# Gated-MLP layers of a six-layer transformer on one core: seven half products for three of the projections' parts, layer norm sums on ScalarE, token mixing between the gate tiles

## The reference, cut to what matters

```python
def gmlp_mixer(h, w_in, ln_g, ln_b, w_s, b_s, w_out):
    B, S, _ = h.shape
    z = jax.nn.gelu(h @ w_in)
    u, v = jnp.split(z, 2, axis=-1)
    v = layernorm(v, ln_g, ln_b)
    n = S // GM_CHUNK
    v = v.reshape(B, n, GM_CHUNK, GM_GROUPS, GM_GROUP_DIM)
    mask = jnp.tril(jnp.ones((GM_CHUNK, GM_CHUNK), dtype=bool))
    ws = jnp.where(mask[None], w_s, jnp.zeros_like(w_s))
    sv = jnp.einsum('gts,bnsgd->bntgd', ws, v) + b_s.T[None, None, :, :, None]
    y = u * sv.reshape(B, S, GM_INNER)
    return y @ w_out
```

## Time and profile before

| | |
|---|---|
| median of 3 runs | 2519.59 us (2516.25 to 2520.73) |
| the profiled execution's own time | 2514.01 us |
| its span, first to last instruction | 2512.2 us |
| granted TensorE clock, mean | 0.993 of full |
| PE busy | 2410.5 us, 96% |
| PE's weight loads (PEld) busy | 2040.0 us, 81% |
| DVE busy | 1620.1 us, 64% |
| ACT busy | 528.1 us, 21% |

### The profile page before, as it was taken

One profiled execution on the slowest core, in us unless ns is written; L12 is line 12 of the kernel. 1 busy time (PEld: TensorE's weight loads), 2 busy tenths in 40 slices (PEclk: granted clock), 3 DMA queues, 4 the chain that ended last, 5 costly groups with the idle time before them and its releaser, 6 DMA issues.

```text
span 2512.2 us, 40482 instructions
## 1 busy us (share of the span) xinstructions
PE 2410.5 (96%) x15728; PEld 2040.0 (81%) x15728; DVE 1620.1 (64%) x3367; ACT 528.1 (21%) x1345; POOL 110.9 (4%) x212
## 2 busy tenths in 40 slices
PE   7998999998889999999999799999999999999997
PEld 4466999654669996789998589998789996789997
DVE  4755887447558873426995559964849983425773
ACT  2232010125321102102211322212222212102210
POOL 0000001000000000000110001110001110000000
PEclk9999999999999999999999999999999999999999
DMA  6223557531136565435876158874238874434442
GB/s 238 104 101 131 194 209 261 202 112 34 59 104 228 209 248 195 161 124 204 294 269 241 51 184 291 288 269 151 92 101 314 288 279 162 172 119 143 167 160 68
DMA packets 122363, 453.46 MB, mean 181 GB/s; under 512 B 13776, under 2 KB 13904, under 8 KB 121680
## 3 DMA queue, kind: packets, MB, share of 16 engines
q1 hardware_dynamic: 92880, 338.24, 38.1%
q0 software_dynamic: 29312, 112.80, 12.6%
HBM read 449.93 MB, written 1.05 MB: 180 GB/s over the span
## 4 chain that ended last, share of the span: by engine, by line
PE 85%; DVE 9%; ACT 3%; issue 2%; DMA 2%; SPq 0%; POOL 0%; DVEq 0%; ACTq 0%
PE pair L543 59%; PE bank L543 24%; DVE adat L1836 1%; DMA adat<-adaw_dram 1%; DVE att_s L1693 1%; PE bank L829 1%; DVE arena L1688 1%; ACT arena L1210 1%; ACT arena L1222 1%; DVE rstd L1472 1%; DVE h L1475 1%; DVE arena L1780 0%; PE bank L774 0%; DVE arena L2171 0%; DVE arena L2167 0%
## 5 line engine op out<-in xcount | busy, mean ns | idle before, releaser
L543 PE MATMUL pair<-h,ring 128*128 128x256 f32 (+1 forms) x3424 | 639.4, 346 | 9.3 <-issue 4.8
L543 PEld LDWEIGHTS pair<-h,ring 128*128 128x128 f32 x3424 | 567.6, 190 | 71.4 <-issue 7.2
L543 PE MATMUL pair<-arena,ring 128*128 128x128 f32 (+1 forms) x2476 | 388.5, 316 | 4.0 <-issue 2.8
L543 PEld LDWEIGHTS pair<-arena,ring 128*128 128x128 f32 x2476 | 355.2, 193 | 32.1 <-issue 4.4
L543 PE MATMUL bank<-arena 128*128 128x128 f32 (+2 forms) x2584 | 298.0, 279 | 32.7 <-ACT arena L1222 26.6
L543 PEld LDWEIGHTS bank<-arena 128*128 128x128 f32 (+2 forms) x2584 | 274.3, 185 | 67.4 <-ACT arena L1222 36.4
L543 PE MATMUL pair<-ring,h 128*128 128x512 f32 (+1 forms) x768 | 326.1, 582 | 3.0 <-DVE h L1475 3.0
L543 PE MATMUL pair<-arena 128*128 128x128 f32 (+6 forms) x2530 | 300.5, 283 | 8.1 <-ACT arena L1194 3.6
L543 PEld LDWEIGHTS pair<-arena 128*128 128x128 f32 (+4 forms) x2530 | 262.5, 185 | 40.9 <-issue 20.5
L543 PEld LDWEIGHTS pair<-ring,h 128*128 128x128 f32 x768 | 142.1, 191 | 168.5 <-issue 159.8
L1836 DVE CUSTOM_DVE_ANT_0 adat<-adat,crow,cols 128x1024 f32<-128x1024 f32 x192 | 244.2, 1278 | 50.0 <-DMA adat<-adaw_dram 50.0
(11 more groups left out here) (232 smaller groups left out, 2162.1 us busy)
## 6 DMA issues: line engine op xcount, KB each, us to landing
ring<-stream_dram SPq DMA_DIRECT2D x638, 512.0 KB, 4.4
adat<-adaw_dram POOLq DMA_DIRECT2D x192, 512.0 KB, 5.1
arena<-gmrows_dram POOLq DMA_DIRECT2D x2, 2560.0 KB, 11.1
arena<-cmpw_dram POOLq DMA_DIRECT2D x1, 2112.0 KB, 9.4
x<-x_in_dram SPq DMA_DIRECT2D x2, 512.0 KB, 4.6
arena<-mem_in_dram SPq DMA_DIRECT2D x1, 1024.0 KB, 12.5
arena<-gmws_dram POOLq DMA_DIRECT2D x2, 512.0 KB, 13.1
out_dram<-h POOLq DMA_DIRECT2D x2, 512.0 KB, 3.8
```

What stands on the lines that cost most here:

```text
L543: return nc.tensor.matmul(out, lhsT, rhs, start=start, stop=stop)
```

## The change

- `gm_v` is of a new kind "V" (`panels`): its first four tiles as before, but taken out of PSUM by ACT, with Gelu and a running sum (`accum_out`) in one; the other twelve as three panels of four tiles, each seven products of four matmuls of 256 columns, on banks 5, 6, 7 and 3. DVE makes four weight sums of 1024 elements a panel and puts the panel together (`panel_out`); ACT copies the first product and applies Gelu with sums.
- The layer norm's sums come from ACT: Gelu's running sums, then four `Square` instructions of 1024 elements with the mean as bias (`deviations`). DVE keeps the small reductions and four passes of 2048 elements.
- `gm_u`: tiles 0 to 3, 14 and 15 as before, 4 to 13 as five pairs (`GM_PAIRED`).
- `gm_out`: three pairs and the tail of two tiles.
- The mixing goes in eight groups of two feature tiles (four matmuls, a whole bank) and stands between gate tiles. DVE's `mixed` (an addition, then a product, of 512 elements each) stands behind each pair's combination and the weight sums two pairs on.

```diff
+            plan += [Linear(f"gm_v{i}", "V", DK, 16, "act"), Linear(f"gm_u{i}", "S", DK, 16, "act"),
+                     Linear(f"gm_out{i}", "S", 16, DK, "dve")]
...
+PANEL = [5, 6, 7, 3]
+GM_PAIRED = range(4, 14, 2)
...
+        GM_MB = (2, 4)
```

PE, in `panels`, for each of the three panels:

```diff
+                    if u == 0:
+                        bank_free(g)
+                    else:
+                        pe.wait_ge(sem("panel_read"), q)
+                    product(5, 0, lambda j: h[:, 2 * j, HALVES[0]], given(0, 0), t)
+                    product(5, 1, lambda j: h[:, 2 * j + 1, HALVES[0]], given(0, 1)).then_inc(sem("panel_first"), 1)
+                    if u == 0:
+                        pe.wait_ge(sem("moving_summed"), MOVING_SUMS[name] + 1)
+                    else:
+                        pe.wait_ge(sem("freed_dve"), FREER[g - 1][1])
+                    product(3, 1, lambda j: upT[1][:, 3, j, :], given(1, 1))
+                    pe.wait_ge(sem("panel_summed"), q + 1)
+                    product(6, 0, lambda j: upT[1][:, 1, j, :], summed(1), t + 4 * lin.K)
+                    product(7, 0, lambda j: upT[1][:, 0, j, :], summed(0))
+                    product(7, 1, lambda j: upT[1][:, 2, j, :], summed(2)).then_inc(sem("panel_mid"), 1)
+                    product(3, 0, lambda j: h[:, 2 * j + 1, HALVES[1]], summed(3)).then_inc(sem("mm_done"), 1)
```

PE, the mixing between gate tiles:

```diff
+                        def mix(m):
+
+                            if m == 0:
+                                pe.wait_ge(sem("gm_v_normed"), 1 + n3)
+                            if m >= 2:
+                                pe.wait_ge(sem("gm_mix_read"), GM_GROUPS * n3 + m - 1)
...
+                            for m in {5: (0,), 7: (1, 2), 9: (3,), 11: (4,), 13: (5,), 15: (6, 7)}.get(n, ()):
+                                mix(m)
```

DVE:

```diff
+                        for u, (_, g) in enumerate(lin.panels):
+                            panel_out(u, g)
+                            if u == 0:
+                                panel_weights(2)
...
+                        V.tensor_scalar(mean, total, -1.0 / GM_INNER, None, ALU.mult).then_inc(sem("gm_mean"), 1)
+                        up_weights()
+                        up_weights()
+                        dve.wait_ge(sem("gm_sq"), 4 * (1 + n3))
...
+                        for p, (_, _, g) in enumerate(lin.pairs):
+                            if p >= 2:
+                                dve.wait_ge(sem("gm_gated"), len(lin.pairs) * n3 + p - 1)
+                            combined(g, high[:, p % 2]).then_inc(sem("freed_dve"), 1)
+                            if p + 2 < len(lin.pairs):
+                                up_weights()
+                            for m in ((), (0,), (1, 2), (3,), (4,))[p]:
+                                mixed(m)
+                        down_weights(f"gm_out{i}")
+                        down_weights(f"gm_out{i}")
+                        mixed(5)
+                        mixed_sums(0)
+                        down_weights(f"gm_out{i}")
+                        down_weights(f"gm_out{i}")
+                        mixed(6)
+                        mixed(7)
+                        mixed_sums(1)
+                        residual(f"gm_out{i}", f"ffn2_{i}", gain, gate, None, high)
```

More of the change, by code:

```diff
@@ L466, in build @@
         for lin in PLAN.values():
-            if lin.kind == "S":
+            if lin.kind == "V":
+                MOVING_SUMS[lin.name] = n_sums
+                n_sums += 1
+            if lin.kind == "S" and not lin.name.startswith("gm_u"):
                 MOVING_SUMS[lin.name] = n_sums
@@ L627, in linear, with panels, product, given @@
                         t += lin.K * w
-            def seven(name, moving, sums, ready, sums_done, norm=None):
+            def panels(name, ready):
+                lin = PLAN[name]
+                t, g = lin.tile0, lin.g0
+                for tt in range(TT):
+                    bank_free(g + tt)
+                    for k in range(lin.K):
+                        ready(tt, k, 0)
+                        last = mm(banks[USED[g + tt][0]][:, :], h[:, k, HALVES[tt]], tile(t + 4 * k, 4), k == 0,
+                                  k == lin.K - 1)
+                        release(last, tt == 1 and k < lin.K - 1, t + 4 * k)
+                    last.then_inc(sem("mm_done"), 1)
+                for u, (t, g) in enumerate(lin.panels):
+                    q = u + len(lin.panels) * (name != "gm_v0")
+                    own = panelW[u % 2]
+                    def product(bank, slot, move, weights, free=None):
+                        for j in range(lin.K // 2):
+                            ins = mm(banks[bank][:, slot * TOK:slot * TOK + TOK], move(j), weights(j), j == 0,
+                                     j == lin.K // 2 - 1)
+                            if j == 0 and free is not None:
+                                release(ins, True, free)
+                        return ins
+                    def given(a, e):
+                        return lambda j: tile(t + (2 * a + e) * lin.K + 2 * j, 2)
+                    def summed(m):
+                        return lambda j: own[:, m, 2 * j:2 * j + 2, :].rearrange("p a q -> p (a q)")
+                    if u == 0:
[14 more added lines that the diff above has]
+                    product(3, 0, lambda j: h[:, 2 * j + 1, HALVES[1]], summed(3)).then_inc(sem("mm_done"), 1)
@@ L631, in seven @@
+            def seven(name, moving, sums, ready, sums_done, norm=None, after=None):
                 lin = PLAN[name]
@@ L725, in seven @@
                     t += lin.K * len(ns)
+                    if after is not None:
+                        after(ns[-1])
             def norm_part(name, k):
```

216 lines of the change are left out of this document (149 added, 67 removed).

## The result

| | before | after |
|---|---|---|
| median of 16 runs each, same chip | 2517.53 us (2514.51 to 2523.21) | 2523.34 us (2518.49 to 2527.62) |
| span of the profiled execution | 2512.2 us | 2522.8 us |
| granted TensorE clock, mean | 0.993 | 0.986 |
| first gated-MLP layer | 165.13 us | 166.70 us |
| second gated-MLP layer | 165.13 us | 167.42 us |

A forecast was written before the change was run, and what follows sets the result against it. PE was taken to bound the layers. Per layer, 18.0 us less work against 15.3 us of waits gave -5.4 us in two layers; clock falls added 11.0, so +5.6 on 2519.6: 2525.2 us, range 2511 to 2532.

The forecast's parts named there:

- PE work: Shorter matmul work: value panels 4.9 us, gate tiles 3.3, output tiles 3.9, mixing 5.9; 18.0 us less a layer.
- panels' waits: Value stage: panels 2 and 3 each wait 0.4 us for DVE's `panel_read`, 0.8 us a layer.
- layer norm: Before mixing group 0: the layer norm ends 0.2 us late for PE, 3.4 us if squares take 2.0 us.
- group 2: Mixing group 2, behind gate pair 6 and 7: PE waits 4.45 us for DVE's first read of a mixing bank.
- group 3: Mixing group 3, behind gate pair 8 and 9: PE waits 5.34 us for DVE, with nothing to cover it.
- `gm_out`: group 6, group 7, moving sums: First output pair: PE waits 2.7 us for group 6, 1.2 for group 7, 0.6 for the second moving sums; 4.5 together.
- clock, by subtraction: Three falls to half clock a layer, behind the long waits: 1.9, 1.9 and 1.7 us, 5.5 a layer, 11.0 in all.
- The prediction's sign that this stage would be 5 us shorter: Value stage: listed among the signs that would show the forecast right, 5 us shorter.
- Rival 4: Layer norm on ACT late, by squares at 2.0 us or table changes: 3.4 us a layer more, 2532 us; chance 0.04.
- Rival 1: The waits come but the clock stays: price 0, sum -5.4 us, 2514.2 us, not slower; chance 0.20.
- Rival 2: DVE is ahead of PE: without any wait two layers save 36 us, 2483.6; half the waits, 2500; chance 0.09.
- Rival 3: The slab ring runs short, panels and output pairs each 1 us late: two layers lose 12 us more, 2537; chance 0.10.

The follow-up runs named there:

- both orders: Changed kernel with DVE's reads of mixing groups 0 to 4 earlier, groups 5 to 7 ahead of output weight sums, PE's group 6 one tile earlier: 2484.12 us, ratio 0.9880.
- sooner reads: Changed kernel with DVE's reads of mixing groups 0 to 4 put one behind each gate pair, instead of none, 0, then 1 and 2: 2494.21 us, ratio 0.9917.
- waits filled: Changed kernel with PE's waits at mixing groups 2 and 3 and the first output pair filled with 50 unread matmuls a layer: 2514.36 us, ratio 0.9986.
- second trace: One more execution each of the kernel before and the changed kernel, nothing edited: 2518.29 us and 2522.71 us.
- tail alone: Changed kernel with DVE's groups 5 to 7 ahead of output weight sums and PE's group 6 one tile earlier, other reads left late: 2515.34 us, ratio 0.9988.
- mixing later: Changed kernel, DVE's program kept, PE's mixing groups 2 to 4 one gate pair later and 5 to 7 behind the last: 2503.40 us, ratio 0.9942.
- gates whole: Changed kernel with all sixteen gate tiles as whole products and DVE's reads of groups 0 to 4 right behind the layer norm: 2494.21 us, ratio 0.9913.

## Why the prediction was right

**The ledger of a layer.** Idle times in brackets count from a modelled end; a wait is read more sharply from the spacing of starts, at 0.2234 us a matmul, or 0.1117 a record. Group 2: 1053.93 - (1048.59 + 8 x 0.1117) = 4.45 us. Group 3: 1068.23 - (1061.92 + 0.89) = 5.42. `gm_out`: 1097.64 - (1093.70 + 12 x 0.1117) = 2.60, then 1098.97 - (1097.64 + 0.22) = 1.11. PE's work without waits comes from the kernel with both orders: 149.21 less 0.45 at each of two panels and 0.88 at the second moving sums (both from spacings too) is 147.43 us.

| term, us a layer | predicted | measured |
|---|---|---|
| PE work | -18.0 | 147.43 - 165.13 = -17.7 |
| panels' waits | 0.8 | 0.9 |
| layer norm | 0.2 | 0 |
| group 2 | 4.45 | 4.45 |
| group 3 | 5.34 | 5.42 |
| `gm_out`: group 6, group 7, moving sums | 2.7, 1.2, 0.6 | 2.60, 1.11, 0 |
| clock, by subtraction | 5.5 | 4.8 and 5.5 |
| sum | +2.8 | +1.57 and +2.29 |

- **What bounds the kernel**: held. In all versions the layer's length is PE's work and PE's waits; DVE's own work of 94 us a layer is the same in the change (166.70 us), in the sooner reads (154.52) and in both orders (149.21).
- **PE's work**: 17.7 of 18.0. A pair of output tiles lasts 12.50 us where 12.51 was taken. Most of the rest is in the value stage, 51.57 us, where the terms gave 55.38 - 4.9 + 0.8 = 51.3. The prediction's sign that this stage would be 5 us shorter left out the panels' waits: by its own terms 4.1, and 3.8 came.
- **Waits**: all in their places but the last at `gm_out`, the two long ones within 0.1 us. They could be had from the trace of before because each operation of the new sequence already had a row there.
- **Layer norm**: the squares at 1.14 us (1.2 taken, 0.5 to 2.0 bounded). PE waits for nothing, since the chain is 0.8 us early where 0.2 late was worked out. Rival 4 is out.
- **The third wait at `gm_out`** was forecast at 0.6 us and is missing in the change. It is there (0.50 us idle) with the waits filled, and in both orders. The fall of the clock ahead of it slows PE down long enough for DVE to come first. DVE's last moving sum ends at 1101.70:

```profile
1101.01 0.69 DVE L1742 TENSOR_TENSOR arena<-arena 128x512 f32<-128x512 f32 x1
```

PE needs it after 18 records, which from 1098.97 would be 1100.98 at full clock; at half clock only 15 records fall into the stretch up to 1102.21. So the gross cost of the clock, 4.8 to 5.5 us a layer, and the net one, 3.8 to 4.5, differ mostly by this hidden wait. Without the clock's term the ledger gives 161.9 us a layer. The filled layers are 162.88: the hidden wait is 0.8 of the difference (by the spacing of starts), and the matmuls of groups 2 and 3, which take 0.99 and 1.00 us there instead of 0.89, are 0.2.

- **The clock**: three falls a layer, all six there. 11.0 us were taken for two layers; by subtraction they cost 10.3, net of the hidden wait 8.4 in the traces and 9.1 in the runs. The waits of 4.3 to 5.3 us had a fall behind them in every trace; that the third would have one too was argued from idle times of 2.97 and 2.10 us, which was thinner than it looked (last section). By the Trainium skill's rule (TensorE: Matmul & The Clock Gate, HAM oscillation) bursts with long gaps between start at the lower clock, and the trace agrees at the four gaps of 4.29 and 5.25 us. The section speaks of gaps longer than a length that it gives, so the prediction put it too widely. The shorter gaps at `gm_out` had a fall each time too, those of the last section in half of the cases. Without the clock the change would have been faster than before, as the filled version shows. Rival 1 put that case at -5.4 us; the filled layers are 4.5 us shorter than before and the ratio gives 3.5, less by the hidden wait. That its 2514.2 us and the measured 2514.36 all but coincide is luck, since the forecast's base lay higher.
- **Rival 2**, DVE ahead of PE: out, though its price was right. It gave 36 us less without any wait; with both orders the two layers are 31.8 us shorter and still wait 1.8 us each, which makes 35.4. By the ratio the kernel gains 30 us, so its 2484.12 beside the rival's 2483.6 is a closer match than the price earned.
- **Rival 3**, the ring: out. In the first layer of the change DVE's weight sums wait for PE, never for a transfer; DMA's share is 0.51 at most.
- **The sum**: the two layers of the profiled execution are 3.9 us longer (in the second trace of the change 4.4), 5.6 were forecast, and by the ratio the kernel is 5.5 slower. That the last two agree to 0.1 us is luck. The layers stay 1.2 to 1.7 us below the forecast, and something outside them, where it put nothing, makes up for it. Chance stretches there vary by more than that. But the traces show a candidate, PE's idle time without a releaser in the part between the two layers (total, times, longest), before and after:

```profile
PE pair L543 <- issue: 1.5, 4, 0.6
...
PE pair L573 <- issue: 4.0, 5, 2.1
```

It is 1.5 and 2.1 us in the two traces of the kernel before, 4.0 and 5.0 in the two of the change and 2.7 to 4.5 in the six of edited kernels. What it comes from, and whether it accounts for the rest of the 5.5, stays open.

What the ledger does not say, and the experiments do: of 14.5 us of waits 12.7, and with them all of the clock's cost, were a matter of where five reads stand in DVE's program and one group in PE's. The prediction treated the order as given; it had all the numbers to see that weight sums needed two pairs later stood in front of a read that PE needed at once.

Not tried: the panels or the output pairs alone, since both need another plan of banks. Their worth is read from the traces only.

## What to carry to other kernels

When work of the bounding engine is cut and the helper engine gets more to do, walk through the helper's program at each point where the bounding engine will wait, and put what frees a bank ahead of what prepares a later step. The same helper work made PE wait 14.5 us a layer in one order and 1.8 in another (with one of PE's own groups a gate tile earlier). If a wait of some us on TensorE can't be removed, price the slow clock behind it too; 50 matmuls a layer that nobody reads gave back 9 us here, but mending the order gave 36.

## What the runs showed of the hardware beyond that

Behind the short idle times, a fall of the clock is chance, and the same program shows it in one execution and not in the next. Three short idle times stand in all ten traces, the same to 0.01 us (the first three rows):

| idle time of PE | stretch at half clock behind it in | none in |
|---|---|---|
| 2.97 us, near 20 | before, change, both orders, tail alone, mixing later | the other five |
| 2.10 us, near 115 | before, change, both orders, gates whole, tail alone | the other five |
| 2.02 us, near 1440 | change, gates whole, mixing later, both second traces | the other five |
| 4.29 to 5.26 us, groups 2 and 3 | all 12 (change twice, tail alone) | none |
| 2.44 + 0.84 us or 2.45 + 0.53, `gm_out` | all 6 (change twice, sooner reads) | none |
| 4.67 + 0.84 us, `gm_out` | both (mixing later) | none |

A fourth short idle time, 2.15 us near 656 with shorter ones of 0.5 to 1.1 us on both sides of it, had a stretch in nine traces and none in the gates whole.

The part between the two gated-MLP layers, which the experiments leave alone, takes 972.1 to 977.1 us in the four traces of edited or changed kernels with the stretch near 1440, and 967.6 to 970.3 in the four without: some 4 us, mostly by chance, out of a spread between runs of the change of 9 us (2518.49 to 2527.62). Up to 2 us of it can be the idle time without a releaser named above, which varies too. The length of a stretch varies too. Behind the waits at `gm_out` the 34 records that come next took 5.54 us with a stretch of 3.41 us, and 6.97 with one of 6.83 (mixing later). A stretch that is absent from one profile, or present, is thus no evidence for a change of a few us; the length of a stage at clock 1.00, equal to 0.01 us in both layers, is.
